# A two-block transformer kernel on one core: split input transfers, input squares on GpSimd, warm-up matmuls and a later row sum at the start

## The chip, the cores and the metric

One core of a Trainium2 chip runs the kernel. The metric is the device time of one execution in microseconds (us), median of several; lower is better. The kernel before takes 1696.99 us, median of 3 runs (1696.12 to 1697.86).

## The reference, cut to what matters

Two transformer blocks of depth 2 run one after the other on x of 256 rows by 1024 columns, all in float32. The change touches only the first operations of the first layer:

```python
def rms_norm(x, g):
    xf = x.astype(jnp.float32)
    y = xf * lax.rsqrt(jnp.mean(xf * xf, axis=-1, keepdims=True) + NORM_EPS)
    return (y * g.astype(jnp.float32)).astype(x.dtype)

def hybrid_layer(x, ...):
    hn = rms_norm(x, ln1)
    proj = hn @ w_in                      # 256x1024 by 1024x(3 attention kinds, gates)
    ...                                   # MoBA, mLSTM and window attention on slices of proj
    x = x + jnp.concatenate([y_moba, y_mlstm, y_swa], axis=-1) @ w_out
    u = rms_norm(x, ln2) @ w_up
    return x + jnp.square(jax.nn.relu(u)) @ w_down
```

## The kernel before, in words

**Data.** x lies transposed in SBUF as 8 chunks of 128 columns by 256 rows. Every weight is cut into units of up to 1024 columns on 128 partitions. Two units make a slab of 1 MB, one transfer, and slabs go through 3 raw buffers. `PLAN` lists the units in the order of use.

**Splits.** A float32 product is made of three passes at the float32r rate: hi by hi, hi by lo, lo by hi. For weights, `act_split` (L381, ScalarE) writes the high part of a unit into one of 4 ring slots, and `dve_split` (L390, VectorE) subtracts it from the raw unit to get the low part. A unit's slot is free when TensorE has counted it in `units_used`. For the input, `act_chunk` (L440) multiplies a chunk of x with the gain ln1 and rounds it (high part), and `dve_chunk` (L455) makes the low part from x and the high part. The normalising factor is not in there: it is applied later, as a factor `rstd` of each row, when a group of columns leaves PSUM.

**Groups of w_in.** The columns of w_in form groups: `G1[0]` has 264 columns (gates of the mLSTM and its q), then come `G_K`, `G_MOBA`, `G_SWA`, `G_X`, `G_V` with up to 512. A unit holds two chunks of such a group, so each group takes 4 units: units 0 to 3 are the first group (528 columns each), units 4 to 7 `G_K`, units 8 to 11 `G_MOBA`, unit 12 begins `G_SWA`. `pe_group` waits for the low part of each unit, runs its 12 matmuls (2 chunks, 2 row tiles, 3 passes; L404 to L406), and calls `after(n)` behind the n-th unit of the group.

**Row sums.** The squares of the 8 chunks are summed into `sumsq` (at the start: squares on ScalarE L447, additions on VectorE L467). `pe_rsum` (L505) sums over partitions with a matmul against ones, `dve_ms` (L512) makes mean plus eps, `pool_norm` (L521, GpSimd) raises it to the power -0.5 into `rstd`. ScalarE then evicts the first group with that factor (L1114). In layer one `pe_rsum` stands behind unit 1, that is `after(1)` of the first group.

**What follows on each queue in order** (layer one, before):
- TensorE: units 0, 1, row sum, units 2, 3, 4, then transposes of the evicted first group (conv input L881 and gates L890), units 5, 6, 7, the t5 table's matmul (L1003), unit 8, second conv transposes, 9, 10, gate columns and decay (L901, L909, L910), 11, decay, 12.
- ScalarE: 8 chunks, units 0 and 1, 8 squares, units 2 to 6, wait for `rstd`, eviction of group one, unit 7, copy of the transposed conv input, exp and log of the gates, units 8 to 10.
- VectorE: 8 chunks, units 0, 1, 7 additions, units 2, 3, 4, mean, units 5, 6, 7, gates (L1264 to L1269), 8 conv taps (L1304, L1309), unit 8, a scan of the gates (L1274 to L1282), units 9, 10, copy of the t5 row (L1438), unit 11, 8 taps, units 12, 13.
- SyncE issues x, 4 small constants and three slabs, then slab 3 when units 0 and 1 are split, slab 4 when units 2 and 3 are, then 13 transfers of constants, then slab 5. GpSimd has `pool_norm`, then the rope tables once the constants are in (L1567, L1570), then the t5 transfers.

Of the kernel before, what the change touches and what calls it, by code (L numbers as in the profile page):

```python
# [175 lines left out]
def build(nc, a, out):  # L176
    ctx = ExitStack()
    with ctx:
# [60 lines left out]
        def over(name, shape, dt=F32):  # L239
# [83 lines left out]
        slab_in = [sem(f"slab_in{i}") for i in range(RAW)]  # L323
        names = """x_in base_in const_in na_skewed0 na_skewed1 t5_row t5_out t5_turned t5_in bias_in stored
            unit_hi unit_lo units_used act_chain dve_chain
# [173 lines left out]

        def pe_rsum(pe, b):  # L500
            bank, n, before = rsum_fill(b)
# [133 lines left out]
        def dve_down(dve, b, n_units, scale, to, gain):  # L635
            for n in range(DC):
# [3 lines left out]
                if to is not None:  # L640
# [4 lines left out]
        X1, X2 = OUT_HALF // 2 + OUT_HALF + DC, 3 * DC  # L645
        X_DONE = DEPTH * (X1 + X2)
        blk = ctx.enter_context(nc.Block())
        BASE = (("pcol1", pcol1), ("ident", ident), ("neg_half", half), ("ones_m", ones_m))
        CONSTS = ((pcol2, "pcol2"), (onehot, "onehot"), (rope_c, "rope_c"), (rope_s, "rope_s"), (mask_m, "mask_m"),
                  (mask_s, "mask_s"), (pick, "pick"), (mask_n, "mask_n"), (ones, "ones"))  # L650
        n_const = len(CONSTS) + 4
# [4 lines left out]
        def _(sp):  # L656
            sp.dma_start(x[:, :, :], a["x"]).then_inc(s["x_in"], 16)
            for name, dst in BASE:
                sp.dma_start(dst[:], a[name]).then_inc(s["base_in"], 16)
            for j in range(RAW):  # L660
                sp.dma_start(raw[j][:, :], a["slabs"][j]).then_inc(slab_in[j], 16)
            for j in range(RAW, SLABS):
# [208 lines left out]
        def pe_layer1(pe, b, l):  # L871
# [105 lines left out]
            for g, (c0, w) in enumerate(G1[:G_V]):  # L977
                def after(n):
                    if g == 0 and n == 1:
                        pe_rsum(pe, b)  # L980
                    if g in (G_K, G_K + 1) and n == 0:
                        wait(pe, value(b, "z_act", 2 * g))
                        turn_tiles(f["conv", g - G_K], z1, ZLQ + (g - G_K) * 2 * P)
                        if g == G_K:
                            turn_gates()
                    if g == G_MOBA and n == 2:
                        gate_columns()
                        decay(0)
# [4 lines left out]
                    if g == G_X and n == 2:  # L993
# [7 lines left out]
                if g == G_K and l == 0:
                    pe.wait_ge(s["const_in"], 16 * n_const)
                    nc.tensor.matmul(sc[0][0:SW, :], t5_tab[:, :], onehot[:, :], start=True, stop=True)\  # L1003
                        .then_inc(sc_full[0], 1)
            out_banks = outs1(b)
# [252 lines left out]
        def dve_layer1(dve, b, l, next_gain):  # L1258
# [162 lines left out]
            for g, (c0, w) in enumerate(G1[:G_V]):  # L1421
                n = len(wide_units("", c0, w))
                b.unit += n
                if g == 0:
                    dve_split(dve, b, b.unit - n + 2 + RING - 1)
                    dve_ms(dve, b)
                    f = fills1(b, l)
                if g == G_K:
# [7 lines left out]
                if g == G_MOBA and l == 0:  # L1436
                    dve.wait_ge(sc_full[0], f["t5"][0])
                    nc.vector.tensor_copy(t5_rel[:, :], sc[0][0:SW, :]).then_inc(s["t5_row"], 1)  # L1438
                if g == G_MOBA:
                    dve_split(dve, b, b.unit - n + RING)  # L1440
                    taps(1)
                    dve_split(dve, b, b.unit - n + RING + 2)
                    gate_columns()
                    decay(0)
                if g == G_SWA:
                    if l == 0:
                        dve.wait_ge(s["const_in"], 16 * n_const)
                        for i in range(DEPTH):
# [701 lines left out]
        def _(act):  # L2150
            b = Book()
            act.wait_ge(s["x_in"], 16)
            act.wait_ge(s["base_in"], 16 * len(BASE))
            gain = pcol1[:, 0, C_LN1:C_LN1 + DC]
            for n in range(DC):
                act_chunk(act, b, act_a, gain, n)
            act_split(act, b, 2)
            for n in range(DC):
                act_square(act, b, n)
            act_split(act, b, RING)  # L2160
            for l in range(DEPTH):
# [6 lines left out]
        def _(dve):  # L2168
            b = Book()
            dve.wait_ge(s["x_in"], 16)  # L2170
            dve.wait_ge(s["base_in"], 16 * len(BASE))
            gain = pcol1[:, 0, C_LN1:C_LN1 + DC]
            for n in range(DC):
                dve_chunk(dve, b, act_a, gain, n)
            dve_split(dve, b, 2)
            for n in range(DC):
                dve_square(dve, b, n)
            dve_split(dve, b, RING)
            for l in range(DEPTH):
# [5 lines left out]
        def _(pool):  # L2185
            b = Book()
            pool.wait_ge(s["base_in"], 16 * len(BASE))
            for l in range(DEPTH):
# [5 lines left out]
def constants():  # L2194
    f = np.float32
    c = {"ident": np.eye(P, dtype=f), "neg_half": np.full((P, 64), -0.5, f), "ones": np.ones((LSTM, S), f),
         "ones_m": np.ones((P, P), f)}
    inv = f(10000.0) ** (-np.arange(0, HD, 2, dtype=f) / f(HD))
# [88 lines left out]
```

## Time and profile before

| what | value |
|---|---|
| median of 3 runs | 1696.99 us (1696.12 to 1697.86) |
| span of the profiled execution, first to last instruction | 1695.1 us |
| difference of the median to that span | 1.9 us |
| TensorE busy | 1669.9 us (99%) |
| VectorE, ScalarE, GpSimd busy | 1235.2, 992.3, 186.5 us |
| DMA | 313.99 MB, mean 185 GB/s |
| granted TensorE clock, mean | 1.000 |

The profiled execution has its span alone on record; the 1.9 us between it and the median of the runs are launch and end, in which this change does nothing. A busy share counts overlapping matmuls as busy, so it says where TensorE had work and not how fast it went: for that one takes start to start distances of matmuls in the timeline.

### The profile page before, as it was taken

How to read it: one execution, taken by the hardware profiler on the slowest of the kernel's cores; microseconds unless marked ns; L12 is line 12 of the kernel's file. 1: busy time of each engine (PE TensorE's matmuls, PEld its weight loads, DVE VectorE, ACT ScalarE, POOL GpSimd, SP SyncE). 2: the span in 40 equal slices, each digit the busy share in tenths (PEclk: the TensorE clock that was granted, in tenths of full speed). 3: DMA queues.
4: the chain of work that ended last, by engine and by line, in shares of the span. 5: the costliest groups of instructions: out<-in, count | busy, mean ns of one | idle time of the engine just before them, and what ended most of it. 6: DMA issues, size and time to landing. Idle time of an engine off the chain costs nothing.

```text
span 1695.1 us, 25641 instructions
## 1 busy us (share of the span) xinstructions
PE 1669.9 (99%) x9966; PEld 1448.0 (85%) x9966; DVE 1235.2 (73%) x1985; ACT 992.3 (59%) x1664; POOL 186.5 (11%) x170
## 2 busy tenths in 40 slices
PE   7999999999999999999999999999999999999999
PEld 5788888878888888888878988888888887898888
DVE  7777765767776568776776877767786677778874
ACT  5676654567665455554576655545554467755542
POOL 2621000162100000000511000000000231100000
PEclk9999999999999999999999999999999999999999
DMA  7625565542656555556523555555555642445553
GB/s 284 196 101 194 192 208 193 216 141 101 243 192 207 193 197 189 185 201 253 191 100 131 193 177 196 198 201 195 179 196 202 246 172 103 147 175 198 197 200 125
DMA packets 62024, 313.99 MB, mean 185 GB/s; under 512 B 22686, under 2 KB 24354, under 8 KB 25295
## 3 DMA queue, kind: packets, MB, share of 16 engines
q1 hardware_dynamic: 60382, 303.93, 50.5%
q0 software_dynamic: 1232, 4.22, 0.8%
q10 hardware_dynamic: 288, 4.19, 0.7%
q8 instruction: 80, 1.31, 0.3%
q14 instruction: 42, 0.34, 0.1%
HBM read 311.25 MB, written 7.36 MB: 188 GB/s over the span
## 4 chain that ended last, share of the span: by engine, by line
PE 90%; ACT 5%; DVE 3%; issue 1%; DMA 0%; SPq 0%; DVEq 0%; ACTq 0%
PE acc L415 45%; PE acc L417 23%; PE acc L404 4%; PE acc L405 4%; PE acc L406 4%; ACT w_hi L381 2%; DVE w_lo L390 1%; PE acc L424 1%; PE acc L426 1%; PE acc L425 1%; PE acc L821 1%; PE tp L807 1%; PE sc L796 1%; ACT work L846 1%; PE acc L571 0%
## 5 line engine op out<-in xcount | busy, mean ns | idle before, releaser
L390 DVE TENSOR_TENSOR w_lo<-raw,w_hi 128x1024 fp32r<-128x1024 f32 (+1 forms) x564 | 680.1, 1213 | 278.5 <-ACT w_hi L381 276.8
L381 ACT ACTIVATE w_hi<-raw 128x1024 fp32r<-128x1024 f32 (+1 forms) x564 | 583.4, 1038 | 187.4 <-PE acc L417 120.4
L415 PE MATMUL acc<-act_a,w_hi 128*128 128x512 f32 x1440 | 505.8, 396 | 1.2 <-DVE w_lo L390 1.2
L415 PE MATMUL acc<-hidden,w_hi 128*128 128x512 f32 x1216 | 421.8, 392 | 0.0
L417 PE MATMUL acc<-act_a,w_lo 128*128 128x256 f32 x1440 | 401.7, 279 | 0.0
L417 PE MATMUL acc<-hidden,w_lo 128*128 128x256 f32 x1216 | 339.2, 279 | 0.0
L415 PEld LDWEIGHTS acc<-act_a,w_hi 128*128 128x128 f32 x1440 | 269.8, 187 | 70.1 <-issue 9.2
L417 PEld LDWEIGHTS acc<-act_a,w_lo 128*128 128x128 f32 x1440 | 271.4, 188 | 0.1
L415 PEld LDWEIGHTS acc<-hidden,w_hi 128*128 128x128 f32 x1216 | 227.6, 187 | 51.0
L589 ACT COPY part<-acc 128x256 f32<-128x256 f32 x272 | 101.4, 373 | 282.9 <-PE acc L417 281.9
L415 PE MATMUL acc<-act_b,w_hi 128*128 128x512 f32 x688 | 239.4, 392 | 0.0
L417 PEld LDWEIGHTS acc<-hidden,w_lo 128*128 128x128 f32 x1216 | 229.2, 189 | 0.0
L417 PE MATMUL acc<-act_b,w_lo 128*128 128x256 f32 x688 | 192.7, 280 | 0.0
L415 PEld LDWEIGHTS acc<-act_b,w_hi 128*128 128x128 f32 x688 | 128.7, 187 | 28.3
L404 PE MATMUL acc<-w_hi,act_a 128*128 128x512 f32 (+2 forms) x352 | 134.9, 383 | 12.5 <-DVE w_lo L390 12.5
L405 PE MATMUL acc<-w_lo,act_a 128*128 128x512 f32 (+2 forms) x352 | 131.6, 374 | 0.0
L406 PE MATMUL acc<-w_hi,act_a 128*128 128x512 f32 (+2 forms) x352 | 131.5, 374 | 0.0
L417 PEld LDWEIGHTS acc<-act_b,w_lo 128*128 128x128 f32 x688 | 130.0, 189 | 0.1
L521 POOL TENSOR_TENSOR rstd<-ms,neg_half 128x2 f32<-128x2 f32 x10 | 12.4, 1242 | 1026.6 <-DVE ms L512 1026.6
L440 ACT ACTIVATE act_a<-x_res,pcol 128x256 fp32r<-128x256 f32 x64 | 31.8, 507 | 104.7 <-DVE x_res L603 92.5
L404 PEld LDWEIGHTS acc<-w_hi,act_a 128*128 128x128 f32 x352 | 67.3, 191 | 27.9 <-issue 16.0
L406 PEld LDWEIGHTS acc<-w_hi,act_a 128*128 128x128 f32 x352 | 67.3, 191 | 11.7
(224 smaller groups left out, 2056.4 us busy)
## 6 DMA issues: line engine op xcount, KB each, us to landing
raw<-in_slabs SPq DMA_DIRECT2D x282, 1024.0 KB, 4.8
na_skew<-in_rpb SPq DMA_DIRECT2D x32, 128.0 KB
na_bias<-na_skew ACTq DMA_DIRECT2D x2, 2048.0 KB, 8.4
t_skew<-t_by_distance POOLq DMA_DIRECT2D x2, 1024.0 KB, 13.8
t_bias<-t_skew POOLq DMA_DIRECT2D x1, 2048.0 KB, 10.6
x_res<-in_x SPq DMA_DIRECT2D x1, 1024.0 KB, 4.9
out_x<-x_res SPq DMA_DIRECT2D x8, 128.0 KB, 4.8
prow<-in_prow SPq DMA_DIRECT2D x1, 518.0 KB
```

Source lines behind the costliest of these rows:

```text
L381: nc.scalar.activation(w_hi[u % RING][:, 0:n], raw[j % RAW][:, (u % 2) * HALF:(u % 2) * HALF + n], ACT.Copy).then_inc(s["unit_hi"], 1)
L390: nc.vector.tensor_tensor(w_lo[u % RING][:, 0:n], raw[j % RAW][:, (u % 2) * HALF:(u % 2) * HALF + n], w_hi[u % RING][:, 0:n].bitcast(F32), ...
L404: nc.tensor.matmul(to, xh, wh, start=first and i == 0, stop=False)
L405: nc.tensor.matmul(to, xh, wl, start=False, stop=False)
L406: mm = nc.tensor.matmul(to, xl, wh, start=False, stop=last and i == n - 1)
L415: nc.tensor.matmul(bank[:, :], wh, src[:, c + i, :, :].rearrange("p i s -> p (i s)"), start=first and i == 0, stop=False, skip_group_check ...
L417: mm = nc.tensor.matmul(bank[:, S:2 * S], wl, src[:, c + i, 0, :], start=False, stop=last and i == n - 1, skip_group_check=True)
L424: nc.tensor.matmul(to, wh, src[:, c, 0, :], start=first, stop=False, skip_group_check=True)
L425: nc.tensor.matmul(to, wh, src[:, c, 1, :], start=False, stop=False, skip_group_check=True)
L426: return nc.tensor.matmul(to, wl, src[:, c, 0, :], start=False, stop=last, skip_group_check=True)
L440: nc.scalar.activation(to[:, n, 0, :], x[:, n, :], ACT.Identity, scale=gain[:, n:n + 1])\
L589: nc.scalar.copy(part[n % 2][:, :], acc[bank][:, 0:S]).then_inc(s["part_ready"], 1)
```

## The change: what it does

- x comes in 4 transfers of 2 chunks, issued by ScalarE; pcol1 (gains) goes first on SyncE, then the first six units in own transfers, with ident between them. `ones_m`, `neg_half` and `ones` are now filled by GpSimd instead of loaded.
- ScalarE and VectorE make two chunks, then one unit, four times over, instead of 8 chunks, 2 units, 8 squares, 2 units.
- The 4 squares (2 chunks each, 512 elements per partition), 3 additions of that size and one of 256 run on GpSimd, in `sq_x`.
- TensorE runs 12 matmuls of `ones_m` into a free bank before its first wait for data.
- In layer one the row sum stands behind unit 5 (was 1), the transposes of the first group behind unit 6 (was 4), and the t5 matmul behind unit 9 (was 7). VectorE takes units 4, 5, 6 ahead of the mean (was unit 4), waits for the constants at `decay(0)` and no longer ahead of the gate scan, and copies the t5 row in `G_SWA`.

```diff
 def act_split(act, b, to):
-                if u % 2 == 0:
-                    act.wait_ge(slab_in[j % RAW], (j // RAW + 1) * 16)
+                if u < 2 * RAW:
+                    act.wait_ge(unit_in[u], 16)
+                elif u % 2 == 0:
+                    act.wait_ge(slab_in[j % RAW], j // RAW * 16)
...
 def _(sp):
-            sp.dma_start(x[:, :, :], a["x"]).then_inc(s["x_in"], 16)
-            for name, dst in BASE:
-                sp.dma_start(dst[:], a[name]).then_inc(s["base_in"], 16)
-            for j in range(RAW):
-                sp.dma_start(raw[j][:, :], a["slabs"][j]).then_inc(slab_in[j], 16)
+            sp.dma_start(pcol1[:], a["pcol1"]).then_inc(s["pcol_in"], 16)
+            for u in range(2 * RAW):
+                n, c = width_of(u), u % 2 * HALF
+                sp.dma_start(raw[u // 2][:, c:c + n], a["slabs"][u // 2, :, c:c + n]).then_inc(unit_in[u], 16)
+                if u == RAW:
+                    sp.dma_start(ident[:], a["ident"]).then_inc(s["base_in"], 16)
...
 def pe_layer1(pe, b, l): (after(n))
-                    if g == 0 and n == 1:
+                    if g == 0 and n == 1 and l:
                         pe_rsum(pe, b)
-                    if g in (G_K, G_K + 1) and n == 0:
+                    if g == G_K and n == 1 and not l:
+                        pe.wait_ge(s["set_done"], 3)
+                        pe_rsum(pe, b, f["rsum"])
+                        pe.wait_ge(s["base_in"], 16)
+                    if g in (G_K, G_K + 1) and n == (0 if l or g > G_K else 2):
                         wait(pe, value(b, "z_act", 2 * g))
                         turn_tiles(f["conv", g - G_K], z1, ZLQ + (g - G_K) * 2 * P)
...
+                    if g == G_MOBA and n == 1 and l == 0:
+                        pe.wait_ge(s["const_in"], 16 * n_const)
+                        nc.tensor.matmul(sc[0][0:SW, :], t5_tab[:, :], onehot[:, :], start=True, stop=True)\
+                            .then_inc(sc_full[0], 1)
...
 def dve_layer1
-                    dve_split(dve, b, b.unit - n + 2 + RING - 1)
+                    dve_split(dve, b, b.unit - (n - 2 if l else 0) + RING - 1)
                     dve_ms(dve, b)
...
                     if l == 0:
-                        dve.wait_ge(s["const_in"], 16 * n_const)
+                        dve.wait_ge(s["set_done"], 3)
                     gates_sum()
...
 def _(pe):
-            pe.wait_ge(s["base_in"], 16 * len(BASE))
+            pe.wait_ge(s["set_done"], 1)
+            for i in range(WARM):
+                nc.tensor.matmul(tp[1][:, 0:P], ones_m[:, :], ones_m[:, :], start=True, stop=True)
...
 def _(act):
+            for k in range(DC // 2):
+                act.dma_start(x[:, 2 * k:2 * k + 2, :], a["x"][:, 2 * k:2 * k + 2, :]).then_inc(x_in[k], 16)
+            act.wait_ge(s["set_done"], 3)
+            nc.scalar.activation(esink[:, 0, :], half[:, 0:T], ACT.Identity)
+            act.wait_ge(s["pcol_in"], 16)
...
 def _(dve):
-            for n in range(DC):
-                dve_chunk(dve, b, act_a, gain, n)
-            dve_split(dve, b, 2)
-            for n in range(DC):
-                dve_square(dve, b, n)
-            dve_split(dve, b, RING)
+            for k in range(DC // 2):
+                dve.wait_ge(x_in[k], 16)
+                dve_chunk(dve, b, act_a, gain, 2 * k)
+                dve_chunk(dve, b, act_a, gain, 2 * k + 1)
+                dve_split(dve, b, k + 1)
...
 def _(pool):
+            nc.gpsimd.memset(ones_m[:, :], 1.0).then_inc(s["set_done"], 1)
+            nc.gpsimd.memset(half[:, :], -0.5).then_inc(s["set_done"], 1)
+            nc.gpsimd.memset(ones[:, :], 1.0).then_inc(s["set_done"], 1)
+            for k in range(DC // 2):
+                xs = x[:, 2 * k:2 * k + 2, :]
+                pool.wait_ge(x_in[k], 16)
+                nc.gpsimd.tensor_tensor(sq_x[:, 2 * k:2 * k + 2, :], xs, xs, ALU.mult).then_inc(s["sq_ready"], 2)
+                if k:
+                    pool.wait_ge(s["sq_ready"], 2 * k + 2)
+                    if k > 1:
+                        pool.wait_ge(s["sq_step"], k - 1)
+                    nc.gpsimd.tensor_tensor(sq_x[:, 0:2, :], sq_x[:, 0:2, :], sq_x[:, 2 * k:2 * k + 2, :], ALU.add)\
+                        .then_inc(s["sq_step"], 1)
+            pool.wait_ge(s["sq_step"], DC // 2 - 1)
+            nc.gpsimd.tensor_tensor(sumsq[:, :], sq_x[:, 0, :], sq_x[:, 1, :], ALU.add).then_inc(s["sq_added"], DC - 1)
```

## Rows read from the trace of the kernel before

**Rows 1.** The page: busy time of each engine, its share, instructions.
```profile
PE 1669.9 (99%) x9966; PEld 1448.0 (85%) x9966; DVE 1235.2 (73%) x1985; ACT 992.3 (59%) x1664; POOL 186.5 (11%) x170
```
**Rows 2.** TensorE's waits over the whole span: us in total, times, longest.
```profile
PE acc L404 <- DVE w_lo L390: 12.5, 1, 12.5
```
**Rows 3.** Timeline, first 30 us, other engines: start us, us, what.
```profile
0.74 0.40 SPq L657 DMA_DIRECT2D x_res<-in_x  x1
...
3.08 1.40 SPq L661 DMA_DIRECT2D raw<-in_slabs  x3
...
8.46 3.26 DVE L455 SCALAR_TENSOR_TENSOR act_a<-x_res,pcol,act_a 128x256 fp32r<-128x256 f32 x8 [8.46 <-ACT act_a L440]
...
11.67 1.33 DVE L390 TENSOR_TENSOR w_lo<-raw,w_hi 128x528 fp32r<-128x528 f32 x2
...
24.98 0.47 DVE L1264 TENSOR_SCALAR gate<-tp,pcol 4x256 f32<-4x256 f32 x1 [0.50 <-PE tp L890]
...
29.28 1.00 POOL L1567 TENSOR_TENSOR rope_gc<-rope_c,prow 128x256 f32<-128x256 f32 x1 [8.35 <-DMA prow<-in_prow]
```
**Rows 4.** Timeline of TensorE: units 0 to 4 at first and last passes, t5, 9, 12.
```profile
12.48 0.56 PE L404 MATMUL acc<-w_hi,act_a 128*128 128x264 f32 x1 [12.48 <-DVE w_lo L390]
...
17.68 0.30 PE L406 MATMUL acc<-w_hi,act_a 128*128 128x264 f32 x1
...
18.18 0.37 PE L404 MATMUL acc<-w_hi,act_a 128*128 128x264 f32 x1
...
21.16 0.39 PE L404 MATMUL acc<-w_hi,act_a 128*128 128x512 f32 x1
...
23.68 0.39 PE L406 MATMUL acc<-w_hi,act_a 128*128 128x512 f32 x1
...
33.06 1.02 PE L1003 MATMUL sc<-onehot,t_tab 33*8 33x512 f32 x2
...
37.24 0.47 PE L404 MATMUL acc<-w_hi,act_a 128*128 128x512 f32 x1
...
47.78 0.50 PE L404 MATMUL acc<-w_hi,act_a 128*128 128x512 f32 x1
```
**Rows 5.** DMA issues of the first 12 us: KB each, median us to landing.
```profile
raw<-in_slabs SPq DMA_DIRECT2D x3, 1024.0 KB, 7.8
x_res<-in_x SPq DMA_DIRECT2D x1, 1024.0 KB, 4.9
```
**Rows 6.** Timeline of VectorE and GpSimd, from 64.6 us.
```profile
64.60 1.37 DVE L390 TENSOR_TENSOR w_lo<-raw,w_hi 128x1024 fp32r<-128x1024 f32 x1 [1.30 <-ACT w_hi L381]
64.85 1.58 POOL L1597 TENSOR_TENSOR qk_b<-z,rope_gs 128x192 f32<-128x192 f32 x1
65.89 2.15 DVE L1337 TENSOR_TENSOR qk<-qk,qk_b 128x1536 f32<-128x1536 f32 x1
66.40 1.83 POOL L1597 TENSOR_TENSOR qk_b<-z,rope_gs 128x64 f32<-128x64 f32 x1
```
**Rows 7.** GpSimd additions and products: groups, 60 to 110 us; L477 min/median/max ns.
```profile
L1606 POOL TENSOR_TENSOR qk<-qk,qk_b 128x1024 f32<-128x1024 f32 x1 | 2.4, 2362 | 0.0
...
L1621 POOL TENSOR_TENSOR lstm_q<-lstm_h 128x256 f32<-128x256 f32 x2 | 1.2, 614 | 0.1
...
L477 POOL TENSOR_TENSOR sumsq<-sumsq,sq_tile x14: 732/743/1477, 123.8 to 433.3; 128x256 f32<-128x256 f32 x14
```
**Rows 8.** Timeline of VectorE at the same place of layer two.
```profile
317.51 0.15 DVE L512 TENSOR_SCALAR ms<-tp 128x2 f32<-128x2 f32 x1
...
321.27 1.37 DVE L390 TENSOR_TENSOR w_lo<-raw,w_hi 128x1024 fp32r<-128x1024 f32 x1 [0.96 <-ACT w_hi L381]
323.00 0.47 DVE L1264 TENSOR_SCALAR gate<-tp,pcol 4x256 f32<-4x256 f32 x1 [0.36 <-PE tp L890]
...
327.62 1.22 DVE L390 TENSOR_TENSOR w_lo<-raw,w_hi 128x1024 fp32r<-128x1024 f32 x1
...
331.61 3.48 DVE L390 TENSOR_TENSOR w_lo<-raw,w_hi 128x1024 fp32r<-128x1024 f32 x3
```

More of the change, by code:

```diff
@@ L262, in build @@
         lstm_q = sb("lstm_q", [P, T, LSTM * HD], offset=xT_at)
+        sq_x = sb("sq_x", [P, DC, S], offset=hk1_at)
         o[0] = hidden0
@@ L323, in build @@
         slab_in = [sem(f"slab_in{i}") for i in range(RAW)]
-        names = """x_in base_in const_in na_skewed0 na_skewed1 t5_row t5_out t5_turned t5_in bias_in stored
+        unit_in = [sem(f"unit_in{u}") for u in range(2 * RAW)]
+        names = """x_in0 x_in1 x_in2 x_in3 pcol_in base_in set_done sq_step const_in na_skewed0 na_skewed1 t5_row t5_out t5_turned t5_in bias_in stored
             unit_hi unit_lo units_used act_chain dve_chain
@@ L339, in build @@
         sc_full = [s["sc_full0"], s["sc_full1"]]
+        x_in = [s[f"x_in{k}"] for k in range(DC // 2)]
         act_chain, dve_chain = s["act_chain"], s["dve_chain"]
@@ L498, in bcast_fill, with pe_rsum @@
             return next_tp(b, (s["rbc_ready"], b.mark("bcast")))
-        def pe_rsum(pe, b):
-            bank, n, before = rsum_fill(b)
+        def pe_rsum(pe, b, fill=None):
+            bank, n, before = rsum_fill(b) if fill is None else fill
             wait(pe, before)
@@ L646, in build @@
         X_DONE = DEPTH * (X1 + X2)
+        WARM = 12
         blk = ctx.enter_context(nc.Block())
-        BASE = (("pcol1", pcol1), ("ident", ident), ("neg_half", half), ("ones_m", ones_m))
         CONSTS = ((pcol2, "pcol2"), (onehot, "onehot"), (rope_c, "rope_c"), (rope_s, "rope_s"), (mask_m, "mask_m"),
-                  (mask_s, "mask_s"), (pick, "pick"), (mask_n, "mask_n"), (ones, "ones"))
+                  (mask_s, "mask_s"), (pick, "pick"), (mask_n, "mask_n"))
         n_const = len(CONSTS) + 4
@@ L999, in pe_layer1 @@
                 if g == 0:
+                    r = None if l else rsum_fill(b)
                     f = fills1(b, l)
[L1001 to L1004, printed above, removed]
+                    f["rsum"] = r
             out_banks = outs1(b)
@@ L1443, in dve_layer1 @@
                     gate_columns()
+                    if l == 0:
+                        dve.wait_ge(s["const_in"], 16 * n_const)
                     decay(0)
@@ L1446, in dve_layer1 @@
                     if l == 0:
-                        dve.wait_ge(s["const_in"], 16 * n_const)
+                        dve.wait_ge(sc_full[0], f["t5"][0])
+                        nc.vector.tensor_copy(t5_rel[:, :], sc[0][0:SW, :]).then_inc(s["t5_row"], 1)
                         for i in range(DEPTH):
@@ L2151, in _ @@
             b = Book()
-            act.wait_ge(s["x_in"], 16)
-            act.wait_ge(s["base_in"], 16 * len(BASE))
-            gain = pcol1[:, 0, C_LN1:C_LN1 + DC]
-            for n in range(DC):
-                act_chunk(act, b, act_a, gain, n)
-            act_split(act, b, 2)
-            for n in range(DC):
-                act_square(act, b, n)
-            act_split(act, b, RING)
+            for k in range(DC // 2):
[3 more added lines that the diff above has]
+            act.wait_ge(s["pcol_in"], 16)
+            gain = pcol1[:, 0, C_LN1:C_LN1 + DC]
+            for k in range(DC // 2):
+                act.wait_ge(x_in[k], 16)
+                act_chunk(act, b, act_a, gain, 2 * k)
+                act_chunk(act, b, act_a, gain, 2 * k + 1)
+                act_split(act, b, k + 1)
+            b.mark("sq_ready", DC)
+            b.mark("sq_added", DC - 1)
             for l in range(DEPTH):
@@ L2169, in _ @@
             b = Book()
-            dve.wait_ge(s["x_in"], 16)
-            dve.wait_ge(s["base_in"], 16 * len(BASE))
+            dve.wait_ge(s["pcol_in"], 16)
             gain = pcol1[:, 0, C_LN1:C_LN1 + DC]
-            for n in range(DC):
-                dve_chunk(dve, b, act_a, gain, n)
-            dve_split(dve, b, 2)
-            for n in range(DC):
-                dve_square(dve, b, n)
-            dve_split(dve, b, RING)
+            for k in range(DC // 2):
[3 more added lines that the diff above has]
+                dve_split(dve, b, k + 1)
+            b.mark("sq_ready", DC)
+            b.mark("sq_added", DC - 1)
+            dve.wait_ge(s["base_in"], 16)
             for l in range(DEPTH):
@@ L2186, in _ @@
             b = Book()
-            pool.wait_ge(s["base_in"], 16 * len(BASE))
+            nc.gpsimd.memset(ones_m[:, :], 1.0).then_inc(s["set_done"], 1)
+            nc.gpsimd.memset(half[:, :], -0.5).then_inc(s["set_done"], 1)
+            nc.gpsimd.memset(ones[:, :], 1.0).then_inc(s["set_done"], 1)
+            for k in range(DC // 2):
+                xs = x[:, 2 * k:2 * k + 2, :]
[9 more added lines that the diff above has]
+            nc.gpsimd.tensor_tensor(sumsq[:, :], sq_x[:, 0, :], sq_x[:, 1, :], ALU.add).then_inc(s["sq_added"], DC - 1)
+            pool.wait_ge(s["set_done"], 2)
             for l in range(DEPTH):
@@ L2195, in constants @@
     f = np.float32
-    c = {"ident": np.eye(P, dtype=f), "neg_half": np.full((P, 64), -0.5, f), "ones": np.ones((LSTM, S), f),
-         "ones_m": np.ones((P, P), f)}
+    c = {"ident": np.eye(P, dtype=f), "ones": np.ones((1, SW), f)}
     inv = f(10000.0) ** (-np.arange(0, HD, 2, dtype=f) / f(HD))
```

5 lines of the change are left out of this document (1 added, 4 removed).

## The prediction, made before the changed kernel ran

> **What bounds the kernel now.** First the page: TensorE is busy for 1669.9 of 1695.1 us, 99% [rows 1]. So a change pays by the time it takes from the stretches in which TensorE stands still, and costs what it adds to them. Second, TensorE's waits: the largest, 12.5 us, is the start, for the low part of unit 0 [rows 2]. Third, the timeline of the start. TensorE begins at 12.48; the first 24 passes of 264 columns start 0.226 us apart (12.48 to 17.68, 23 steps), the next 24 only 0.124 us apart (18.18 to 21.16) [rows 4]. That is the lower of the engine's two clocks (1.2 GHz) until 17.9 and the higher (2.4 GHz) after it, though the page's clock line says full speed; it costs 24 x 0.10 = 2.4 us. From 12.48 on TensorE has no wait left in that view before unit 12 at 47.78 [rows 2, 4]. I take unit 12's start as the milestone: whatever it moves by moves the end, since behind it each engine has the same work in the same order.
>
> **Why the new G_K has a chain of its own.** The row sum moves behind unit 5 and the transposes behind unit 6. Behind those transposes only unit 7 is left ahead of unit 8; before, there were three units (5, 6, 7). But unit 8's low part on VectorE stands behind gates and taps. Let E be the end of unit 5, all in us.
> - Row sum and its reading: the four small passes take 0.4 (17.68 to 18.18 less one pass) [rows 4], so the mean starts at E+0.65, an estimate.
> - From the mean to the end of unit 7's split the order is mean, pow on GpSimd, eviction, unit 7's high part, low part. Layer two shows it: 317.51 to 321.27+1.37, 5.1 us [rows 8]. Gates then start at g = E+5.75. TensorE has unit 6 and 1 us of transposes meanwhile and reaches unit 7 at E+4.5: it waits about 1.2 us.
> - Unit 8's split ends at g+5.75 (323.00 to 328.75, the gates and 8 taps, then the split), units 9's at g+9.8 (331.61+1.16) [rows 8]. Unit 7 ends at g+2.75: 3 us of waiting. Unit 8 and the transposes end at g+8.9: 0.9 us more for unit 9.
> - Unit 9 to unit 12 takes 47.78-37.24 = 10.5, and the t5 matmul, which now lies there, 1.0 (33.06 to unit 8) [rows 4]. Unit 12 starts at g+21.35.
> Before, g was 24.98 [rows 3] and unit 12 came at 47.78, so the kernel moves by g' - 26.4 = E - 20.7. The late row sum thus eats 5 us that TensorE did not lose before.
>
> **When unit 5 ends: transfers.** x lands at 0.74+4.9 = 5.64, and the middle one of three slabs (issued at 3.08+0.47) 7.8 later, at 11.3 [rows 3, 5]: 2048 KB in 5.7 us, 360 KB/us. The first quarter of x (256 KB) competes with pcol1 and unit 0 (together 560 KB): it lands (1024-560)/360 = 1.3 us earlier, at 4.4; alone on the wires it would be 3.5. I take 4.5. The Trainium skill (DMA: Bandwidth & Descriptors, "Issuing engines are not separate DMA queues") says transfers from different engines interleave on the same 16 DMA engines, so that a second issuer saves only issue time; by it 4.4, by separate queues 3.5.
>
> **When unit 5 ends: VectorE and GpSimd.** This is the term that decides. Without GpSimd, VectorE would need per step two chunks at 3.26/8 = 0.41 and a 528-column split at 0.66 [rows 3], 1.5 us a unit: TensorE starts at 6.7, unit 4 at 12.65, E = 18.15. But the new squares run on GpSimd beside it, and the trace shows what two such instructions do to each other. At 64.60 VectorE is in a split; GpSimd's product of 192 elements, issued at 64.85, takes 1.58, ending 0.5 after the split. VectorE's next instruction (1536 elements) takes 2.15, though its neighbours run an element per ns, and GpSimd's next, of 64 elements, 1.83: it ends just after that one [rows 6]. They take turns, whole instruction by whole instruction. Both kinds that VectorE runs at the start read two operands in SBUF, as these do. The Trainium skill (SBUF — State Buffer, "Who interferes with whom") speaks against this change: a VectorE instruction with two SBUF inputs and a GpSimd one that reads SBUF exclude each other for a whole instruction. By that rule, the trace agrees (1.83 us for 64 elements).
> GpSimd's work: 256 elements take 0.74 (sum) or 0.61 (square), 1024 take 2.36 [rows 7]; between them 512 take 1.28 and, scaled by 0.61/0.74, 1.06. Sum: 4 x 1.06 + 3 x 1.28 + 0.74 = 8.8 us. VectorE up to unit 4's split: 8 x 0.41 + 4 x 0.66 + 1.16 = 7.1 [rows 3, 8]. Taking turns from 4.55 without a gap, both are through at 4.55+8.8+7.1 = 20.4. In turns: unit 0's split ends at 9.4 (ahead of it two squares, a sum, two chunks), unit 1's at 13.4 to 14.2, unit 2's at 17.7, unit 3's at 19.2. TensorE runs unit 3 to 20.7, then units 4 and 5 (2.75 each, 12 passes, 0.229 apart from 21.16 to 23.68 [rows 4]): E = 26.2. GpSimd is done by 17, so the row sum waits for nothing.
>
> **The other edits.** The 12 warm-up matmuls end near 6 and cost nothing: TensorE has no data then. What they buy is doubtful, since TensorE then pauses until 9.4 and again for some 3 us behind units 0 and 1. Bounds: 0, the higher clock throughout; 2.4, as before. Units 2 and 3 follow five us of nearly steady work, which is where it rose before [rows 4]; I take 0.5. Unit 6's slab is issued at 13.8 and, at 7.8 [rows 5], lands at 22, before its turn at 26. The constants are issued 1 us later than before, so the rope tables (29.28 [rows 3]) fall on unit 7's split and the taps; they take turns there too: 0 to 1.5, I take 0.2 beyond the 1.37 of rows 8. Delayed t5 copy: GpSimd's next product has to wait, its users stand later on VectorE: 0.
>
> **Sum.** 26.2 - 20.7 + 0.2 + 0.5 = +6.2 us: unit 12 at 54.0, span 1701.3, median 1703.2 with the 1.9 us around the span (the median is 1696.99).
>
> **Rivals.**
> - *No mutual exclusion* (ends not slower). If these instructions don't hold each other up, E = 18.15 and the kernel moves by 18.15-20.7 = -2.6; with x early (3.5), -3.6: 1694.4 and 1693.4. Against it: rows 6. It decides if unit 0's split ends before about 7.5. Chance 0.16.
> - *VectorE keeps the turn.* GpSimd gets through only when VectorE waits for a semaphore. Unit 4 starts at 12.65, but the sum is ready only near 22.3 (13.4 + what is left of 8.8 + one split), where TensorE waits at 18.15: +1.6, 1698.6. For it: VectorE's queue is full at the start. Against: in rows 6 it was full too. Chance 0.12.
> - *The clock falls again.* As forecast, but pauses of 3 us before units 1 and 8 put TensorE at the lower clock at the start and in G_K: +2.4 less the 0.5, and a unit at 0.45 a pass costs 2.7 more: 1705 to 1708. For it: the lower clock after the idle start in rows 4. Chance 0.13.
> - Forecast, 1700.5 to 1705.5: 0.59.
>
> **Numbers.** 0.2% of 1697 is 3.4 us, about what a measurement tells from no change. Faster by more needs the first rival and an early x: 0.11. Same (1693.6 to 1700.4): the rest of it, the second rival, and a forecast whose GpSimd terms come out 3 us smaller: 0.25. Slower 0.64. The range 1694 to 1707 takes in most of all four; the forecast's own is 1700.5 to 1705.5.
>
> **What would show it.** First real matmul near 9.4 (6.7 by the first two rivals). On VectorE, chunks shown as 1 to 1.7 us instead of 0.48, each beside a GpSimd instruction; GpSimd's squares done near 17. Unit 4 near 20.7, row sum near 26.4, TensorE waits of about 1, 3 and 1 us at units 7, 8, 9 for w_lo. Wrong I am if the chunks stay near 0.41, or if unit 8 comes without a wait.

## The result, and the profile after

The changed kernel takes 1703.44 us, median of 4 runs (1702.68 to 1705.91); the kernel before takes 1696.63 beside it (4 runs). The ratio is 1.0041, 95% interval 1.0029 to 1.0053: slower by 0.4%, as forecast (1703.2). The span of the profiled execution, the fastest of the four, grows from 1695.1 to 1700.9, by 5.8, and unit 12, the milestone, starts at 53.68 instead of 47.78 [rows 4], by 5.9. So the whole loss arises ahead of unit 12, and what follows it is the same work moved.

The page of after, part 1, against [rows 1]: TensorE is busy for 8 us more, of which 5.5 are the warm-up (its 12 matmuls stand in the profile as 24).

```profile
PE 1677.9 (99%) x9990; PEld 1452.8 (85%) x9990; DVE 1239.6 (73%) x1978; ACT 989.8 (58%) x1657; POOL 195.9 (12%) x181
```

TensorE's waits in after, 0 to 60 us (us in total, times, longest), against [rows 2]:

```profile
PE acc L409 <- DVE w_lo L395: 5.6, 4, 2.7
PE acc L409 <- ACT z L1126: 3.8, 1, 3.8
```

One wait of 12.5 us has become several. The timeline of TensorE in after shows where (start us, us, what; the bracket is the idle time before and what ended it), against [rows 4]:

```profile
0.98 5.49 PE L2156 MATMUL tp<-ones_m 128*128 128x128 f32 x24 [0.98 <-POOL ones_m L2206]
9.13 0.39 PE L409 MATMUL acc<-w_hi,act_a 128*128 128x264 f32 x1 [2.65 <-DVE w_lo L395]
...
13.43 0.59 PE L409 MATMUL acc<-w_hi,act_a 128*128 128x264 f32 x1 [1.81 <-DVE w_lo L395]
...
17.19 0.39 PE L409 MATMUL acc<-w_hi,act_a 128*128 128x264 f32 x1 [0.75 <-DVE w_lo L395]
...
20.21 0.40 PE L409 MATMUL acc<-w_hi,act_a 128*128 128x512 f32 x1
...
25.69 0.50 PE L510 MATMUL tp<-ones_m,sumsq 128*128 128x2 f32 x4
...
30.39 0.50 PE L409 MATMUL acc<-w_hi,act_a 128*128 128x512 f32 x1 [0.44 <-DVE w_lo L395]
...
37.22 0.77 PE L409 MATMUL acc<-w_hi,act_a 128*128 128x512 f32 x1 [3.80 <-ACT z L1126]
...
41.92 0.48 PE L409 MATMUL acc<-w_hi,act_a 128*128 128x512 f32 x1
...
53.68 0.50 PE L409 MATMUL acc<-w_hi,act_a 128*128 128x512 f32 x1
```

These are the warm-up, units 0, 1, 2 and 4, the row sum, units 7, 8, 9 and 12. TensorE has its first data 3.35 us earlier than before, but it waits again ahead of units 1 and 2. Unit 4 starts at 20.21 against 21.16 [rows 4]: of the early start 0.95 is left. From unit 4 to unit 12 it then takes 33.47 us instead of 26.62, 6.85 more: the row sum that now lies there (0.36), the waits at units 7 and 8 (4.24), the lower clock within unit 8 (some 1.5: its start to unit 9's is 4.70, before 3.22), and small gaps.

VectorE in after, same columns, against [rows 3]. Two chunks take 2.68 instead of 0.82, and a split of 528 columns 1.23 to 1.77 instead of 0.66, until GpSimd is done at 16.57; the next four splits in a row (unit 3's of 528 columns and three of 1024; the row gives the shape of the first only) then take 4.10, which is what they need alone:

```profile
4.67 1.09 DVE L460 SCALAR_TENSOR_TENSOR act_a<-x_res,pcol,act_a 128x256 fp32r<-128x256 f32 x2 [4.67 <-ACT act_a L445]
7.85 1.23 DVE L395 TENSOR_TENSOR w_lo<-raw,w_hi 128x528 fp32r<-128x528 f32 x1 [2.08 <-ACT w_hi L386]
9.00 2.68 DVE L460 SCALAR_TENSOR_TENSOR act_a<-x_res,pcol,act_a 128x256 fp32r<-128x256 f32 x2
11.60 1.77 DVE L395 TENSOR_TENSOR w_lo<-raw,w_hi 128x528 fp32r<-128x528 f32 x1
...
17.06 0.87 DVE L460 SCALAR_TENSOR_TENSOR act_a<-x_res,pcol,act_a 128x256 fp32r<-128x256 f32 x2
17.85 4.10 DVE L395 TENSOR_TENSOR w_lo<-raw,w_hi 128x528 fp32r<-128x528 f32 x4
26.23 0.16 DVE L517 TENSOR_SCALAR ms<-tp 128x2 f32<-128x2 f32 x1 [4.28 <-PE tp L510]
29.11 1.23 DVE L395 TENSOR_TENSOR w_lo<-raw,w_hi 128x1024 fp32r<-128x1024 f32 x1 [2.73 <-ACT w_hi L386]
30.26 0.47 DVE L1276 TENSOR_SCALAR gate<-tp,pcol 4x256 f32<-4x256 f32 x1
...
35.85 1.22 DVE L395 TENSOR_TENSOR w_lo<-raw,w_hi 128x1024 fp32r<-128x1024 f32 x1
```

GpSimd in after, the counterpart: seven instructions without a gap from 7.47 to 16.57. The row at 26.54 is the power; the one at 29.77 is the first of the rope tables, beside the split and the taps:

```profile
4.05 1.04 POOL L2212 TENSOR_TENSOR sq_x<-x_res 128x512 f32<-128x512 f32 x1 [2.80 <-DMA x_res<-in_x]
7.47 1.04 POOL L2212 TENSOR_TENSOR sq_x<-x_res 128x512 f32<-128x512 f32 x1 [2.38 <-DMA x_res<-in_x]
8.59 1.63 POOL L2217 TENSOR_TENSOR sq_x<-sq_x 128x512 f32<-128x512 f32 x1
...
15.84 0.73 POOL L2220 TENSOR_TENSOR sumsq<-sq_x 128x256 f32<-128x256 f32 x1
26.54 0.71 POOL L526 TENSOR_TENSOR rstd<-ms,neg_half 128x2 f32<-128x2 f32 x1 [9.97 <-DVE ms L517]
29.77 1.16 POOL L1579 TENSOR_TENSOR rope_gc<-rope_c,prow 128x256 f32<-128x256 f32 x1 [2.52 <-DMA prow<-in_prow]
```

### The profile page after: what moved, and what is told of

Its sections match the earlier page's. It is cut to its first block, busy times and chain, and to the rows that moved or that the text cites. A ratio compares the mean times of both kernels' runs of the same rounds, so it can differ in the third digit from the quotient of the medians.

```text
span 1700.9 us, 25698 instructions
## 1 busy us (share of the span) xinstructions
PE 1677.9 (99%) x9990; PEld 1452.8 (85%) x9990; DVE 1239.6 (73%) x1978; ACT 989.8 (58%) x1657; POOL 195.9 (12%) x181
## 4 chain that ended last, share of the span: by engine, by line
PE 90%; ACT 5%; DVE 4%; issue 1%; DMA 0%; POOL 0%; SPq 0%; DVEq 0%; ACTq 0%; POOLq 0%
PE acc L420 45%; PE acc L422 23%; PE acc L409 4%; PE acc L410 4%; PE acc L411 4%; DVE w_lo L395 2%; ACT w_hi L386 2%; PE acc L429 1%; PE acc L431 1%; PE acc L430 1%; PE acc L827 1%; PE tp L813 1%; PE sc L802 1%; ACT work L852 1%; PE acc L576 0%
```

## Experiments

Each kernel is the changed one with one edit (e7 to e9 have several). Numbers are medians in us with the ratio to the kernel before, which ran on the same chip each time: 1696.46, 1696.79 and 1696.61 in the three sets. "Later" and "earlier" are against the trace of after unless said otherwise. Two executions of one kernel can differ in the first 20 us, by the moment at which TensorE's clock rises; this comes up several times.

**e1: GpSimd out of the start.** The squares and their sum are left out and a constant takes the place of `sumsq`; so this time is that of a kernel with less work for GpSimd.

```diff
 def _(pool):
-            for k in range(DC // 2):
...
-            nc.gpsimd.tensor_tensor(sumsq[:, :], sq_x[:, 0, :], sq_x[:, 1, :], ALU.add).then_inc(s["sq_added"], DC - 1)
+            nc.gpsimd.memset(sumsq[:, 0:P], 8.0).then_inc(s["sq_ready"], DC)
+            nc.gpsimd.memset(sumsq[:, P:S], 8.0).then_inc(s["sq_added"], DC - 1)
```

> The changed kernel with GpSimd's squares and sums left out: it only fills sumsq with a constant, so the output's first norm is not that of the reference. Nothing but the shared turns between VectorE and GpSimd at the start, and GpSimd's own work, goes. Theory of turns: VectorE's chunks fall from about 1.3 us to 0.41 each, its 528-column splits from 1.2-1.8 to 0.66; unit 0 is still held to 7.2 by its transfer, so TensorE starts at 8.5, unit 4 starts near 14.5 (its transfer landed at 12.2, then 1.06 and 1.2 of splits) instead of 20.2, unit 5 ends at 20 instead of 25.9: 1697.5 us, 6 less than 1703.4. Rival, that transfers and the late row sum alone set the start: 1703.4 as it is, chunks unchanged.

Measured: 1698.7 (11 runs), 1.0015 [1.0006, 1.0024]. VectorE in e1:

```profile
8.79 0.71 DVE L395 TENSOR_TENSOR w_lo<-raw,w_hi 128x528 fp32r<-128x528 f32 x1 [3.23 <-ACT w_hi L386]
9.42 0.87 DVE L460 SCALAR_TENSOR_TENSOR act_a<-x_res,pcol,act_a 128x256 fp32r<-128x256 f32 x2
```

With GpSimd idle the same instructions take 0.87 for two chunks and 0.71 for a split: the turn-taking theory holds. Although unit 0's transfer landed 0.95 later in this execution (at 1700.59 us the slowest of its 11), the row sum comes at 22.48, 3.2 earlier. The median gains 4.7, somewhat less than the 5.9 expected. Part of what is missing shows behind unit 12: transposes at 81.45 wait 0.98 for ScalarE, which they don't in after; e7 to e9 come back to this wait. Of TensorE's waits, those at units 7 and 8 stay, and here the longest bears VectorE's name:

```profile
27.62 0.50 PE L409 MATMUL acc<-w_hi,act_a 128*128 128x512 f32 x1 [0.88 <-DVE w_lo L395]
34.30 0.72 PE L409 MATMUL acc<-w_hi,act_a 128*128 128x512 f32 x1 [3.67 <-DVE w_lo L395]
```

**e2: the row sum back behind unit 1, the transposes behind unit 4.** Squares stay on GpSimd.

```diff
-                    if g == 0 and n == 1 and l:
+                    if g == 0 and n == 1:
                         pe_rsum(pe, b)
-                    if g in (G_K, G_K + 1) and n == (0 if l or g > G_K else 2):
+                    if g in (G_K, G_K + 1) and n == 0:
...
-                    dve_split(dve, b, b.unit - (n - 2 if l else 0) + RING - 1)
+                    dve_split(dve, b, b.unit - n + 2 + RING - 1)
```

> The changed kernel with the row sum back behind unit 1, the transposes back behind unit 4 and VectorE's mean back behind unit 4's split; squares stay on GpSimd, transfers and warm-up stay. Theory (the late row sum makes a chain that TensorE waits for at units 7 and 8): the sums are ready at 16.6, unit 1 ends at 16.2, so 0.4 us of waiting there and none at units 7, 8 and 9; unit 12 starts 26.6 us behind unit 4 as in the kernel before, at 46.8 instead of 53.7: 1696.5 us, 6.9 less. Rival, that turns and transfers at the start are the whole loss: 1703.4 or a little more for the earlier wait.

Measured: 1697.93 (11 runs), 1.0008 [1.0000, 1.0017], 5.5 below after where 6.9 was expected. All of TensorE's waits from 10 to 60 us in e2:

```profile
13.35 0.59 PE L409 MATMUL acc<-w_hi,act_a 128*128 128x264 f32 x1 [1.29 <-DVE w_lo L395]
16.54 1.01 PE L510 MATMUL tp<-ones_m,sumsq 128*128 128x2 f32 x4 [0.19 <-POOL sumsq L2216]
37.48 0.50 PE L409 MATMUL acc<-w_hi,act_a 128*128 128x512 f32 x1 [0.27 <-DVE w_lo L395]
```

The waits at units 7 and 8 are gone and GpSimd's sum is ready in time (0.19 of waiting). Unit 12 starts at 49.24, 4.4 earlier, though unit 4 starts 1.9 later (22.08), since the clock rose only near 21 in this execution and the row sum lies ahead of it again. The two losses of the change are thus of about the same size: e2 lies 0.8 below e1, and such a difference is within what two medians of one kernel differ by (e7, below). Together e1 and e2 give back 4.7 + 5.5 = 10.2 us, more than the 6.8 that the change lost. The rest, some 3 us if the two add up, would be what the earlier transfers gain and the losses had covered; that is an argument, and e7, which takes both losses away at once, tests it.

**e3 and e4: units split ahead of the taps.** If the waits at 7 to 9 are VectorE's backlog behind the gates, one unit ahead of the taps moves the wait to unit 9 and three take it away.

```diff
                 if g in (G_K, G_K + 1):
-                    act_split(act, b, b.unit - n + RING)
+                    act_split(act, b, b.unit - n + RING + (1 if g == G_K and l == 0 else 0))
...
                     gates_in()
+                    if l == 0:
+                        dve_split(dve, b, b.unit - n + RING + 1)
                     taps(0)
```

(e4 has 3 in both places.)

> The changed kernel, in layer one only: unit 8 is split (high part and low part) ahead of the copy, gates and taps' place, that is behind unit 7 on ScalarE and between gates and taps on VectorE. Theory (TensorE's wait at unit 8 is a backlog of VectorE's work): unit 8 comes in time but unit 9 then waits about 4 us, for taps, scan and its split: 1703 within 1.5 us, the rest being the clock, which may fall at unit 9 instead. Rival, that only unit 8's place in the order is at fault: 3.8 us of waiting and 1.4 us of low clock go, 1698.5.

> As e3_one_unit_ahead, but units 8, 9 and 10 are all split ahead of the taps. Backlog theory: TensorE then has 9 us of work while VectorE runs 8 taps and the scan (6.5 us); no wait at units 8 to 11 and no fall of the clock: 3.8 + 1.4 us less, about 1698.3 us. Rival, that the waits come from elsewhere (ScalarE's eviction, transfers of slab 5): no gain or a new wait of the same size.

Measured: e3 1705.61 (5 runs), 1.005 [1.0037, 1.0062]; e4 1702.54 (6 runs), 1.0034 [1.0022, 1.0046]. TensorE's waits in e3 from unit 7 on, then the row sum and the waits in e4, with a pass at the lower clock behind the last:

```profile
30.57 0.50 PE L409 MATMUL acc<-w_hi,act_a 128*128 128x512 f32 x1 [0.43 <-DVE w_lo L395]
37.16 0.66 PE L887 MATMUL tp<-ident,z 128*128 128x128 f32 x4 [0.85 <-ACT z L1126]
41.32 0.79 PE L409 MATMUL acc<-w_hi,act_a 128*128 128x512 f32 x1 [3.51 <-DVE w_lo L395]
```

```profile
27.75 0.50 PE L510 MATMUL tp<-ones_m,sumsq 128*128 128x2 f32 x4
32.49 0.50 PE L409 MATMUL acc<-w_hi,act_a 128*128 128x512 f32 x1 [0.48 <-DVE w_lo L395]
50.45 0.48 PE L915 MATMUL tp<-g_u,pick 4*128 4x128 f32 x2 [1.08 <-DVE gcol L1300]
...
52.84 0.63 PE L409 MATMUL acc<-w_hi,act_a 128*128 128x512 f32 x1
```

As to the mechanism both came out: in e3 unit 8 doesn't wait and unit 9 waits 3.51; in e4 no unit from 8 to 12 waits for its split, and from the gates to unit 12 it takes 18.9 instead of 23.4.

As to time both missed. e3's median is 2.6 above the 1703 expected, outside the 1.5 allowed. Its runs differ with the mean granted clock: 1703.29 and 1704.11 at 0.997, which is what the profiled execution of after had, and 1705.61 to 1706.37 at 0.994 to 0.995. So the miss goes with the clock, and at after's clock the forecast holds; what the lower clock fell on in the other three runs no trace shows.

e4 took 1702.54 where 1698.3 was expected. Its profiled execution (1702.57) can be laid beside that of after (1702.68), and there 5.1 of the 5.2 us are missing: 2.06 at the start (units 2 and 3 at the low clock, row sum at 27.75 instead of 25.69); 0.7 between the gates and unit 12, with the pause of 1.08; 1.5 in unit 12, where passes are 0.43 apart (5.36 to unit 13, in after 3.83); and 1.0 behind it, at 83.41, where transposes wait 0.98 for ScalarE as in e1. Four of the other five runs had the same granted clock within 0.001 (0.995 to 0.996) and took 1701.96 to 1703.0; the fifth had 0.999 and took 1701.01.

**e5: no warm-up.** The edit is `WARM = 12` to `WARM = 0`.

> The changed kernel without its 12 warm-up matmuls, all else kept. In the changed kernel's trace the warm-up ends at 6.5, units 0 and 1 are held back by their splits (9.1 and 13.4) whatever the clock, and the low clock of most of units 0 and 1 costs nothing. Theory (the warm-up buys nothing at the end): within 1 us of 1703.4, unit 2 at 17.2, whichever clock it then gets. Rival (the warm-up is what brings the higher clock by unit 2): units 2 and 3 run at 0.22 us a pass, 2.4 us more, 1705.8.

Measured: 1704.22 (5 runs), 1.0042 [1.0029, 1.0054], the same as with it. In e5 TensorE's second unit, at 13.41, ran at the high clock (0.12 between passes), in after at the low one (0.22); by unit 4 they are level (20.19 and 20.21), since in both VectorE sets the start of each of the first three units. The warm-up neither helps nor costs by more than the 1 us that two such medians can differ by.

**e6: all transfers of the start on one queue, in the order of use.** SyncE issues x quarter, unit, x quarter, unit and so on; ScalarE issues none.

```diff
 def _(sp):
-            sp.dma_start(pcol1[:], a["pcol1"]).then_inc(s["pcol_in"], 16)
             for u in range(2 * RAW):
+                if u < DC // 2:
+                    sp.dma_start(x[:, 2 * u:2 * u + 2, :], a["x"][:, 2 * u:2 * u + 2, :]).then_inc(x_in[u], 16)
+                if u == 0:
+                    sp.dma_start(pcol1[:], a["pcol1"]).then_inc(s["pcol_in"], 16)
```

> The changed kernel with all start transfers on SyncE's one queue in the order of use: first quarter of x, pcol1, unit 0, second quarter, unit 1 and so on; ScalarE issues none. Theory (two queues share the wires, so unit 0 and the second quarter of x, asked for at 1.2, land only at 7.2 to 7.5): unit 0 lands near 4.7 and the second quarter near 5.5, TensorE starts at 7 instead of 9.1, and since GpSimd and VectorE then take turns without the pause of 2 us that they had, unit 4 starts 1.0 to 1.8 us earlier: 1702. Rival (the turns alone set unit 4): unit 0 earlier, unit 4 at 20.2 as it was, 1703.4.

Measured: 1704.31 (5 runs), 1.0047 [1.0034, 1.006], where 1702 was expected. The theory fell. ScalarE in after, then in e6, at the moment at which it gets unit 0:

```profile
7.17 0.64 ACT L386 ACTIVATE w_hi<-raw 128x528 fp32r<-128x528 f32 x1 [2.25 <-DMA raw<-in_slabs]
```

```profile
6.76 0.64 ACT L386 ACTIVATE w_hi<-raw 128x528 fp32r<-128x528 f32 x1 [1.85 <-DMA raw<-in_slabs]
```

Unit 0 landed 0.4 earlier. TensorE had it at 8.20 instead of 9.13, but in that execution it stayed at the low clock until 21.2, and the row sum came at 27.07. The order on the queues isn't what holds unit 0 back.

**e7: squares on ScalarE.** ScalarE squares behind unit 4's high part, VectorE adds, the row sum stands behind unit 4, the transposes behind unit 5, and units 8 and 9 are split ahead of the taps.

```diff
 def _(act):
+            act_split(act, b, RING + 1)
+            for k in range(DC // 2):
+                nc.scalar.activation(sq_x[:, 2 * k:2 * k + 2, :], x[:, 2 * k:2 * k + 2, :], ACT.Square)\
+                    .then_inc(s["sq_ready"], 2)
 def pe_layer1
-                    if g == G_K and n == 1 and not l:
+                    if g == G_K and n == 0 and not l:
-                    if g in (G_K, G_K + 1) and n == (0 if l or g > G_K else 2):
+                    if g in (G_K, G_K + 1) and n == (0 if l or g > G_K else 1):
```

> The changed kernel with its three faults mended in turn: squares on ScalarE behind unit 4's high part, the 4 additions on VectorE behind unit 4's low part, GpSimd idle there; row sum behind unit 4 and transposes behind unit 5; units 8 and 9 split ahead of the taps. Transfers as in the changed kernel. Theory: TensorE starts at 8.5 (transfer of unit 0 at 7.2), unit 4 at 14.5, row sum at 17.4, unit 5 at 18, transposes at 21, units 8 and 9 without a wait, unit 12 near 42 against 47.8 in the kernel before and 53.7 in the changed one: 1690.8 us, 0.34% faster than before. Rival (a start that is denser only moves the wait to the first group's eviction or to transfers of slabs 3 to 5): 1695 to 1697.

**e8** is e7 with the one queue of e6.

> e7_act_squares with the transfers of e6_one_queue. Theory: unit 0 lands near 4.7, TensorE starts near 6.5, 2 us ahead of e7_act_squares, and everything behind it moves with it: 1688.8 us. Rival (units 4 and 5, last in the one queue, land no earlier than now and set the pace): as e7_act_squares, 1690.8.

Measured: e7 1694.79 (11 runs), 0.9991 [0.9983, 1.0000]; e8 1694.9 (11 runs), 0.9989 [0.998, 0.9998]. They are 8.65 and 8.54 below after, so taking both losses away works, and e1's and e2's 10.2 add up for the most part (with units 8 and 9 split early besides). But they stay 4.0 and 6.1 above what was expected. The queue again changed nothing. Of e7's 4.0, 1.25 had gone by the row sum (18.65, expected 17.4; the first 13 passes ran at the low clock), and 1.0 went at unit 10, where TensorE waits 0.97 for the low part (36.37). Most of the rest lies behind unit 12. In e7 unit 12 starts at 44.23, 3.5 ahead of before, and yet the span is only 2.1 shorter. The timeline of e7 behind the milestone shows two waits that before doesn't have:

```profile
60.76 0.50 PE L409 MATMUL acc<-w_hi,act_a 128*128 128x512 f32 x1 [0.33 <-DVE w_lo L395]
...
75.52 1.07 PE L887 MATMUL tp<-ident,qk 128*128 128x128 f32 x8 [0.41 <-ACT prob_t L1187]
```

and GpSimd and VectorE around them show why. GpSimd in e7:

```profile
49.94 2.23 POOL L1593 DMA_DIRECT2D t_skew<-t_by_distance  x2 [3.49 <-DMA t_by_distance<-t_rel]
52.19 5.51 POOL L1611 TENSOR_TENSOR qk_b<-z,rope_gs 128x192 f32<-128x192 f32 x8
```

The change had also moved the copy of the t5 row to the group of unit 12. GpSimd issues that table's transfers in order with its other work, so its rope products wait for the copy: in the trace of before they begin at 48.45, here at 52.19, now beside VectorE's means of squares and splits, where they take turns again (VectorE's `msq` takes 1.38, before 0.18).

**e9: e7 with the t5 copy ahead of the second taps.** e7 ran again beside it.

```diff
                 if g == G_MOBA:
                     dve_split(dve, b, b.unit - n + RING)
+                    if l == 0:
+                        dve.wait_ge(s["const_in"], 16 * n_const)
+                        dve.wait_ge(sc_full[0], f["t5"][0])
+                        nc.vector.tensor_copy(t5_rel[:, :], sc[0][0:SW, :]).then_inc(s["t5_row"], 1)
                     taps(1)
```

> As e7 (squares on ScalarE, units 8 and 9 ahead of the taps), but VectorE copies the t5 row ahead of its second set of taps instead of behind unit 12's split. In e7 unit 12 starts 3.5 us earlier than before, yet the kernel ends only 2.1 earlier: GpSimd, held by the late copy, issues the table's transfers at 49.9 and begins its rope products at 52.2 instead of 48.5, and VectorE's instructions beside them take longer (ms of the heads 1.38 against 0.18, a split 1.69 against 1.22). Theory (the late copy takes back part of the gain): rope products begin near 47, waits of TensorE at 60.8 (0.33) and 75.5 (0.41) go, 0.8 to 1.2 us less than e7: 1693.8. Rival (those two waits come from the milestone moving, not from the copy; GpSimd's rope products start later than unit 12 moves anyway): within 0.3 of e7, 1694.8.

> The kernel of e7 a second time, on the same chip and in the same rounds as e9, so that the two can be set beside each other: 1694.8, ratio to before 0.9991. If it comes out over 1 us from that, differences of under 1 us between kernels of different jobs mean nothing.

Measured: e9 1694.07 (11 runs), 0.9986 [0.9977, 0.9995]; e7 again 1695.87 (11 runs), 0.9995 [0.9987, 1.0004]. GpSimd, then VectorE and TensorE in e9:

```profile
44.98 4.67 POOL L1611 TENSOR_TENSOR qk_b<-z,rope_gs 128x192 f32<-128x192 f32 x8
...
54.57 0.18 DVE L1330 TENSOR_SCALAR msq<-ssq 128x24 f32<-128x24 f32 x1
...
74.12 1.09 PE L887 MATMUL tp<-ident,qk 128*128 128x128 f32 x8
```

Rope products begin at 44.98, `msq` is back at 0.18, both waits are gone, and those transposes start 3.2 ahead of before (77.35), the 3.2 that unit 12 has there (44.59). The late copy had eaten the rest. The waits of 0.98 in e1 and e4 are for the same result (`prob_t`) and fit it, but there the copy was not moved to see. e9 is the best version found: 2.5 us faster than before, 9.4 than after. e7's two medians differ by 1.1 us, so differences below about that between sets mean little; e9 and e7 again ran in the same rounds and are 1.8 apart, more than the 0.8 to 1.2 expected. The profiled execution of e7 again waits 1.41 at the same transposes (78.09), the one of e7 0.41, that of e9 not at all.

## Why the prediction was right

**VectorE and GpSimd take turns: right, and its sum nearly so.** Units 0, 1, 2 and 4 were forecast at 9.4, 13.4 to 14.2, 17.7 and 20.7, and came at 9.13, 13.43, 17.19 and 20.21; GpSimd is done at 16.57 (forecast 17). e1 shows the cause. The rivals without exclusion and with VectorE keeping the turn are out: the chunks took 1.34 each, and GpSimd got one instruction through between any two of VectorE's. The first quarter of x was there at 4.05, where 4.5 was taken (3.5 and 4.4 were the two estimates). The one assumption in it that failed did little harm: unit 0 and the second quarter of x were taken as there by the time they were needed, near 5.6, and came at 7.17 and 7.47, so both engines stood idle for 2 us (the brackets at 7.85 and 7.47). That the sum without such a gap was even 0.5 too long is luck: I took 15.9 us of work as strictly in turn, and some 2 us of it ran beside each other (the first square began at 4.05, and from there to unit 4's split, near 19.7, it took 15.6 with 1.7 of it empty).

**The late row sum's chain: the mechanism right, its parts off both ways.** From E (25.69) to the mean it took 0.54, not 0.65. From the mean to the end of unit 7's split it took 4.1 instead of 5.1, because the power took 0.71 and not the 1.61 of layer two, from which the 5.1 was read. This is the forecast's own mechanism, at a place where it was not looked for. In layer two of before the power is issued while VectorE is in a split:

```profile
317.58 1.22 DVE L390 TENSOR_TENSOR w_lo<-raw,w_hi 128x1024 fp32r<-128x1024 f32 x1
...
317.74 1.61 POOL L521 TENSOR_TENSOR rstd<-ms,neg_half 128x2 f32<-128x2 f32 x1 [174.38 <-DVE ms L512]
```

In after the row sum comes so late that VectorE has nothing to do beside it: between the mean (26.23) and unit 7's split (29.11) it is idle, and the power at 26.54 has its turn at once. So the gates began at 30.26, where 31.95 was forecast, and unit 7 waited 0.44 and not 1.2. Then 2.07 were lost again from there to unit 12 (23.42 instead of 21.35). 1.06 of it is the rope tables: I took 0.2 within bounds of 0 to 1.5, and the rows show gates, taps and unit 8's split at 6.81 instead of 5.75 (0.1 of it is a misreading: 327.62 + 1.22 lies 5.84 behind 323.00 [rows 8]). The eight taps take 4.34 there, beside the rope tables, and 3.42 at 43.25, where GpSimd is idle. Another 0.65 is the clock at unit 8; the other 0.4 are small gaps. The wait at unit 8 was 3.80 (forecast 3). That the view names ScalarE's eviction for it is a matter of which semaphore came last: the eviction and the split of unit 8 end at about 37.2 and 37.07, and e1 has the same wait under `w_lo`. In e3 unit 8 starts at 33.42, 2.5 us before that eviction begins (35.88), so it isn't what unit 8 needs. e2 and e4 show that it is the backlog.

**The clock.** TensorE ran at the high level (2.4 GHz) at first, then at the low one (1.2 GHz) from the middle of unit 0 to the end of unit 1, and again in unit 8 behind the wait of 3.80. The windows of after give the granted clock (us, then busy of each engine, then PEclk, DMA share and GB/s):

```profile
12.00:18.00 6.00, 3.82 (x18) 3.51 (x19) 6.00 (x7) 2.12 (x2) 4.35 (x4) 0.62 0.51 195
18.00:24.00 6.00, 6.00 (x37) 5.34 (x36) 3.95 (x4) 1.06 (x1) 0.00 (x0) 1.00 0.75 245
...
36.00:42.00 6.00, 4.78 (x17) 3.88 (x17) 5.86 (x9) 2.72 (x4) 0.00 (x0) 0.72 0.00 0
```

So half of the rival on the clock occurred, beside the forecast and not in its place. At units 0 and 1 it cost nothing, as TensorE waits for VectorE behind them anyway. In unit 8, seven passes 0.43 apart instead of 0.23 cost 1.4 to 1.5, but 0.9 of this lies in the wait for unit 9 that was forecast and so did not occur: unit 9 came at 41.92 without any.

**The other edits.** The warm-up is worth nothing that can be measured (e5). The t5 copy was costed at 0, and in after it is: the transposes at 77.35 before start at 83.25 after, 5.9 later like the milestone. But the cover was the delay itself: as soon as the losses ahead of it were gone (e7) it cost 1.8 us (e9 against e7 again; 0.7 against e7's first median). The forecast called it hidden and did not name that cover.

**The sum.** +6.2 was forecast for the median, +6.8 came (5.8 in the span of the profiled execution). It was the sum of a start 0.5 too late, a chain 1.2 too long, a stretch from the gates on 2.1 too short, and 0.7 set aside for the clock and the rope tables; these cancel to 0.3 at unit 12 (54.0 forecast, 53.68 measured). That they cancel is luck. A result as near as this says less about the parts than each row does.

## What to carry to other kernels

Work moved to GpSimd isn't free when VectorE is on the critical path at that moment: look in the trace for one place where both run on operands in SBUF and read how long each takes there. It cuts both ways: a small step on GpSimd, like the power, takes 0.7 us or 1.6 depending on what VectorE is doing when it is issued. Here the fastest versions (e7, e9) have the squares on ScalarE, though no run moved them alone. Before a small step with a long chain behind it (a row sum, whose reader frees the next engine) is made later, count how many units of work lie between it and the first one that stands behind the chain's end. And where a step is called hidden, write down what hides it, for it comes due when that cover is removed.

## What the runs showed of the hardware that was not expected

- The first transfers land later than their bytes over the rate of the whole would give: the first quarter of x was there at 4.05, unit 0 and the second quarter only at 7.17 and about 7.4, and on one queue instead of two hardly earlier (e6: 6.76 and 7.53). What holds them back is open. In the view of the DMA of after, 0 to 14 us (busy tenths, GB/s of slices of 0.35 us) the rate dips before it reaches its level:

```profile
DMA  0000076989998687999999999999999999531000
GB/s 0 0 0 0 3 116 140 212 256 339 270 143 95 77 148 136 207 316 363 393 409 422 398 404 411 407 414 400 416 429 421 410 398 421 234 129 47 0 0 0
```

- The moment at which TensorE's clock rises differs between executions of the same instructions: e7 had the high level from about 11.4 in one profiled execution and from 14.1 in the other (4.6 us after its first real pass), and after and e4, with the same start, reached the row sum 2.06 apart. In e4 the low level came 2.4 us after a pause of only 1.08. In after, e3 and e4 the runs with the lower mean granted clock took 1 to 3 us more (after: 1705.91 at 0.994 against 1702.68 to 1703.83 at 0.997); in e2 it made no difference (1697.57 to 1698.68 between 0.996 and 0.999).
- The power on 128x2 elements, ten times in each kernel, took 0.69 to 0.71 where no VectorE split was under way when it began, and 1.54 to 1.65 where one was; this holds for all 30 in the traces of before, after and e7. The exclusion thus costs GpSimd up to 0.9 us on an instruction of two elements a partition.
- The page's clock line and the windows can miss a stretch at the low level: the windows of e5 give 1.00 for 6 to 12 us, where the passes of unit 0 start 0.22 apart (9.95, 10.61, 11.27 for every third one). Start to start distances are the safer reading.
